# Second expert stage of a two-block network: down weights loaded with neighbouring rows in one partition, gate and up columns read with a stride

## What is computed

```python
def _moe_swiglu(u, w_router, w_gate, w_up, w_down):       # 256 tokens, 8 experts, top 2
    ...                                                    # tokens sorted by expert
    h = silu(ragged_dot(xs, w_gate, group_sizes)) * ragged_dot(xs, w_up, group_sizes)
    ys = ragged_dot(h, w_down, group_sizes) * top_w
    ...                                                    # summed back by token
```

## Time and profile before

| | us |
|---|---|
| timed runs, median of 3 (lowest, highest) | 2250.08 (2250.03, 2257.03) |
| profiled execution, its own time | 2249.02 |
| its span, first to last instruction | 2247.3 |
| TensorE busy (share) | 2081.7 (93%) |
| VectorE busy | 686.1 (31%) |
| ScalarE busy | 173.9 (8%) |
| GpSimd busy | 165.9 (7%) |
| mean granted TensorE clock | 0.939 |

### The profile page before, as it was taken

How to read it: one execution, slowest core, us unless ns; L and a number is a source line. 1 busy time by engine, 2 the same in 40 slices (tenths; PEclk the granted TensorE clock), 3 DMA queues, 4 the chain that set the end, 5 groups by cost and what they waited for, 6 DMA issues and landing times.

```text
span 2247.3 us, 72263 instructions
## 1 busy us (share of the span) xinstructions
PE 2081.7 (93%) x32971; PEld 1735.1 (77%) x32971; DVE 686.1 (31%) x1542; ACT 173.9 (8%) x280; POOL 165.9 (7%) x203
## 2 busy tenths in 40 slices
PE   6999998999999998998999989888999999989995
PEld 6899867777777776765877667478988989989893
DVE  5774533222222224235423441520110110101105
ACT  1000101000000000100000010020000101000000
POOL 8990000000000000000000000000000000000000
PEclk9977887999999998998999999979999999999997
DMA  9766455999999999334766633149999999999990
GB/s 310 287 242 245 164 201 182 386 393 393 395 395 394 392 395 391 137 113 142 260 251 231 243 131 132 57 174 393 376 379 396 381 384 382 383 393 372 380 396 28
DMA packets 310532, 656.16 MB, mean 292 GB/s; under 512 B 25620, under 2 KB 46644, under 8 KB 310452
## 3 DMA queue, kind: packets, MB, share of 16 engines
q1 hardware_dynamic: 300832, 647.02, 78.3%
q0 software_dynamic: 1456, 5.24, 0.7%
q10 hardware_dynamic: 8164, 2.73, 0.5%
HBM read 653.89 MB, written 1.05 MB: 291 GB/s over the span
## 4 chain that ended last, share of the span: by engine, by line
PE 73%; DMA 19%; DVE 4%; SPq 2%; issue 1%; ACTq 0%; ACT 0%; DVEq 0%
PE ps L1529 72%; DMA ring<-in_moe_w_up_dram 10%; DMA ring<-in_w_down_dram 9%; PE ps L1537 2%; SPq L416 1%; DMA ring<-in_w_ada_dram 1%; DVE hT L868 0%; SPq L329 0%; DMA arena<-in_gm_b_s_dram 0%; ACTq L555 0%; DVE x L941 0%; DVE stat L929 0%; DVE x L1335 0%; DVE x L912 0%; DVE x L910 0%
## 5 line engine op out<-in xcount | busy, mean ns | idle before, releaser
L1529 PE MATMUL ps<-arena,ring 128*64 128x80 f32 (+2 forms) x25216 | 887.9, 232 | 48.8 <-DMA ring<-in_moe_w_up_dram 46.2
L1529 PEld LDWEIGHTS ps<-arena,ring 128*64 128x64 f32 (+1 forms) x25216 | 872.8, 139 | 72.2 <-DMA ring<-in_moe_w_up_dram 50.3
L1529 PE MATMUL ps<-hT,ring 128*128 128x256 f32 x1616 | 363.7, 388 | 3.5 <-DVE stat L1472 1.9
L1529 PEld LDWEIGHTS ps<-hT,ring 128*128 128x128 f32 x1616 | 313.5, 195 | 50.4 <-issue 4.4
L1529 PE MATMUL ps<-ring,arena 128*64 128x512 f32 (+1 forms) x880 | 280.3, 609 | 16.4 <-DMA ring<-in_w_down_dram 15.1
L1529 PE MATMUL ps<-arena 128*128 128x128 f32 (+7 forms) x1296 | 232.9, 346 | 15.8 <-DVE arena L1387 5.6
L1529 PEld LDWEIGHTS ps<-ring,arena 128*64 128x64 f32 (+1 forms) x880 | 107.2, 162 | 171.1 <-issue 168.7
L1529 PEld LDWEIGHTS ps<-arena 128*128 128x128 f32 (+4 forms) x1296 | 160.4, 193 | 67.0 <-issue 41.6
L1274 DVE TENSOR_TENSOR arena<-arena,ps 128x160 f32<-128x160 f32 x88 | 28.3, 322 | 538.2 <-PE ps L1529 538.2
L1529 PEld LDWEIGHTS ps<-csT,ring 128*64 128x64 f32 x3072 | 141.9, 199 | 15.0 <-issue 11.5
L1529 PE MATMUL ps<-csT,ring 128*64 128x1 f32 x3072 | 142.7, 230 | 10.6 <-issue 7.2
(11 more groups left out here) (303 smaller groups left out, 860.6 us busy)
## 6 DMA issues: line engine op xcount, KB each, us to landing
ring<-in_moe_w_gate_dram SPq DMA_DIRECT2D x160, 512.0 KB, 10.0
ring<-in_moe_w_up_dram SPq DMA_DIRECT2D x160, 512.0 KB, 7.2
ring<-in_moe_w_down_dram SPq DMA_DIRECT2D x160, 512.0 KB, 10.2
ring<-in_w_gate_dram SPq DMA_DIRECT2D x32, 2048.0 KB, 20.0
ring<-in_w_up_dram SPq DMA_DIRECT2D x32, 2048.0 KB, 19.7
ring<-in_w_down_dram SPq DMA_DIRECT2D x32, 2048.0 KB, 18.9
ring<-in_w_in_dram SPq DMA_DIRECT2D x18, 2048.0 KB, 12.8
ring<-in_w_ada_dram SPq DMA_DIRECT2D x12, 2048.0 KB, 11.4
```

The source lines that it names most:

```text
L1529: ins = pe.matmul(*args, **kw)
```

## The change

The down matrix goes into the slot in another row order: partition p of a unit now holds the four neighbouring rows c0 + 4p to c0 + 4p + 3, which lie 16 KB in one piece in DRAM, and it is loaded in `SPANS` = 2 transfers of two rows (8 KB) per partition instead of four of one row. Hidden tile f is therefore the features 4q + f, q = 0 to 127, and so gate and up columns of that tile are taken 4 columns apart (16 bytes) from the slot, whose loading stays as it was. In the tail there are two rows per partition, loaded in one transfer as before, and the columns are 2 apart. The freeing of the down slot goes by halves: `FREES` falls from 9 to 7. The branch `second_all` gets the same order (`spread_tiles`).

```diff
-FREES = 2 * PIECES + 1
+SPANS = 2
+FREES = PIECES + 1 + SPANS
...
-        down_piece = [sem(f"down_piece{i}") for i in range(PIECES)]
+        down_piece = [sem(f"down_piece{i}") for i in range(SPANS)]
...
+            def row_spans(w, e, c0, n):
+                return w[bass.ds(e, 1), c0:c0 + n, :].rearrange("o (p k) n -> p (o k) n", p=P)
+
             def load_unit(e, c0, waits):
-                gate, up, down = expert_cols(wg, e, c0, CH), expert_cols(wu, e, c0, CH), expert_rows(wd, e, c0, CH)
+                gate, up, down = expert_cols(wg, e, c0, CH), expert_cols(wu, e, c0, CH), row_spans(wd, e, c0, CH)
...
-                for f in range(PIECES):
-                    sp.wait_ge(*waits(PIECES + 1 + f))
-                    sp.dma_start(down_w[:, f:f + 1, :], down[:, f:f + 1, :]).then_inc(down_piece[f], 16)
+                for h in range(SPANS):
+                    sp.wait_ge(*waits(PIECES + 1 + h))
+                    sp.dma_start(down_w[:, 2 * h:2 * h + 2, :], down[:, 2 * h:2 * h + 2, :]).then_inc(down_piece[h], 16)
...
-                sp.dma_start(tail_down_w, expert_rows(wd, e, c0, TAIL)).then_inc(tail_full["down"], 16)
+                sp.dma_start(tail_down_w, row_spans(wd, e, c0, TAIL)).then_inc(tail_full["down"], 16)
...
+            def column_span(w, f):
+                return w.rearrange("p k (q f) -> p k f q", q=P)[:, :, f, :]
...
-                                      gate_w[:, k, f * P + c * HALF:f * P + (c + 1) * HALF], xT[:, k, 0:cap],
+                                      column_span(gate_w, f)[:, k, c * HALF:(c + 1) * HALF], xT[:, k, 0:cap],
...
-                                          w[:, k, f * P + c * HALF:f * P + (c + 1) * HALF], xT[:, k, 0:cap],
+                                          column_span(w, f)[:, k, c * HALF:(c + 1) * HALF], xT[:, k, 0:cap],
...
-                    for f in range(PIECES):
-                        unit_ready([down_piece[f]], n)
-                        if f % 2 == 0:
-                            pe.wait_ge(q["hid_ready"], i * halves + u * 2 + (f // 2 + 1))
-                        down(down_w, f, False).then_inc(unit_free, 1)
+                    for h in range(SPANS):
+                        unit_ready([down_piece[h]], n)
+                        pe.wait_ge(q["hid_ready"], i * halves + u * 2 + (h + 1))
+                        down(down_w, 2 * h, False)
+                        down(down_w, 2 * h + 1, False).then_inc(unit_free, 1)
```

More of the change, by code:

```diff
@@ L1616, in hT_ready, with spread_tiles @@
                 pe.wait_ge(a_free, na[0])
+            def column_span(w, f):
+                return w.rearrange("p k (q f) -> p k f q", q=P)[:, :, f, :]
+            def spread_tiles(w, rhs, tiles, bank):
+                for i, f in enumerate(tiles):
+                    for k in range(KD):
+                        last = mm(ps[:, bank, i * T:(i + 1) * T], column_span(w, f)[:, k, :], rhs(k),
+                                  start=(k == 0), stop=(k == KD - 1))
+                return last
             def feature_major(w, rhs, tiles, bank, cols=lambda f: f * P, kt=KD, m=P):
@@ L1749, in _, with dense_in @@
             router(w_router, 36)
-            def dense_in(q, gate, up, n, i, per, j):
+            def dense_in(q, gate, up, n, i, per, j, tiles_of=feature_major):
                 for h in range(n // FU):
@@ L1755, in dense_in @@
                         pe.wait_ge(q["silu_done"], i * per + (j + h))
-                    feature_major(gate, h_rhs, (2 * h, 2 * h + 1), 4).then_inc(q["gate_full"], 1)
+                    tiles_of(gate, h_rhs, (2 * h, 2 * h + 1), 4).then_inc(q["gate_full"], 1)
                     if j + h:
                         pe.wait_ge(q["hid_ready"], i * per + (j + h))
-                    feature_major(up, h_rhs, (2 * h, 2 * h + 1), 5).then_inc(q["up_full"], 1)
+                    tiles_of(up, h_rhs, (2 * h, 2 * h + 1), 5).then_inc(q["up_full"], 1)
             def dense_down(q, w, n, i, per, j, unit, opens, closes):
@@ L1809, in second_all @@
                         unit_ready([up_block], i * UNITS + u, PIECES)
-                        dense_in(q, gate_w, up_w, CH, i, S2, 2 * u)
+                        dense_in(q, gate_w, up_w, CH, i, S2, 2 * u, spread_tiles)
                         free(PIECES + 1, unit_free)
                         unit_ready(down_piece, i * UNITS + u)
-                        dense_down(q, down_w, CH, i, S2, 2 * u, u, u == 0, False).then_inc(unit_free, PIECES)
+                        dense_down(q, down_w, CH, i, S2, 2 * u, u, u == 0, False).then_inc(unit_free, SPANS)
                     unit_ready([tail_full["gate"], tail_full["up"]], i)
-                    dense_in(q, tail_gate_w, tail_up_w, TAIL, i, S2, 2 * UNITS)
+                    dense_in(q, tail_gate_w, tail_up_w, TAIL, i, S2, 2 * UNITS, spread_tiles)
                     free(2, tail_free)
```

## The result

The changed kernel takes 2444.0 us (median of 4 runs, 2440.7 to 2444.8) against 2250.1 before: 1.085 times as long, 95% interval 1.083 to 1.088, 194 us slower. The forecast of 2246 us was wrong. The time lies where the first rival put it (2432 for a weight load twice as long), and 4 us beyond the range.

A forecast was written before the change was run, and what follows sets the result against it. Transfers were taken as the bound, TensorE nearly level with them. From 2249.0 us, packets took off 4, freeing, SP and strided loads added 0: 2245.0, or 2246 on the median's scale; range 2237 to 2440.

The forecast's parts named there:

- the first rival: Second expert stage: strided weight loads become TensorE's bound; doubled load gives 2432 us, chance 0.32; 1.5 times, 2285, chance 0.10.
- the strided weights: Gate and up weight loads on TensorE, columns 16 bytes apart: extra cost taken as hidden behind the product, 0 us.
- the slack: TensorE in the second expert stage: 7.3 us per expert that it can lose before the stage slows down.
- middle case: First rival's smaller size: strided load 1.5 times as long, 44.4 ns per instruction, 2285 us; chance 0.10.
- The packets: Down matrix transfers: two rows in one 8 KB packet save 10 ns per pair, 6.7 us, of which 4 us arrive.
- Freeing by halves: Down slot reloaded in two 1 MB halves instead of four 512 KB pieces: hidden by 3 us of margin, cost 0.
- SP's queue: SP issues two transfers fewer per unit, 80 in all, at 345 ns each: off the path, 0 us.
- The tail: Tail weights read with a stride of 8 bytes, two elements to a line: taken as unchanged in all cases.
- The second rival: Down transfers: the pair still travels as two 4 KB packets, or the gain only makes idle time; 2250 us, chance 0.13.

The follow-up runs named there:

- e2_stride: Kernel before with gate and up columns of a unit read 4 apart (2 in the tail), down matrix still loaded in four pieces of 4 KB rows; 2444.0 us.
- e7_full: Changed kernel with gate and up weights of units and tail loaded as one block of 128 columns instead of two of 64, strides kept; 3124.1 us.
- e8_narrow: Changed kernel with only 40 of the 80 token columns streamed in the gate and up products of units and tail; 2447.0 us in one run.

## Why the prediction was wrong

**The step that failed** is the last term of the sum, the strided weights, taken as hidden. I reasoned that a float32 column takes two cycles of the load already, and that this is time enough to reach another address. The runs fit 1.8 ns for each line of 16 bytes touched. With two elements to a line that is the 0.9 ns for each element of the contiguous load, which is why it looks as if it had room; with one element to a line it is twice as much. The load became 2.05 times as long (118 ns against 57.5), beyond the 1.17 from which it shows and the 1.38 from which the stage slows.

The Trainium skill, page "SBUF — State Buffer", section "Door 1: The DMA port swizzle", asks for at least two accesses to a line of 16 bytes; the runs agree, with 61 to 62 ns for a pair at stride 2 and 120 at stride 4. Its following sentence, which lets float32 stride four elements for free, doesn't hold here: two are all but free, three cost a half more, four the double.

**The rival's price** was right in kind. It had 58.8 ns for a strided instruction, 22.8 us per expert and 2432 us; measured were 60.1 ns, 24.7 us and 2444. TensorE's work on an expert grew by 32.5 us (from 82.1 to 114.6) where the rival had 30.1, and the slack took 7.9 off instead of 7.3. Its middle case, 44.4 ns at 1.5 times the load and 2285 us, came with stride 3: 43.7 ns and 2274. The bound 2440 of the range took the doubled load as the worst and left nothing for its pace to be a little above.

**The packets**: 10 ns for each pair was right. The rows of before continue to 309 ns for 8192 bytes, on 16 engines 424 GB/s, and 424 was measured; the packets' own records in the stage have 84, 159 and 309 ns for 2, 4 and 8 KB at their tenth percentile (87, 162 and 314 at the median). Of 6.7 us I let 4 arrive; 5.6 do in the run with contiguous columns (3.2 to 8.3 by its interval, so 4 and 6.7 both fit). In the changed kernel none does, since no wait for a transfer is left that it could shorten: `e2_stride`, without the longer packets, takes the same 2444 us.

**Freeing by halves and SP's queue**: nothing, as taken. **The slack**: 7.9 us against 7.3. **The tail** at stride 2: unchanged, as the rival had it. **The second rival**, that the pair travels as two packets, is refuted by the count.

## What to carry to other kernels

A layout that makes a transfer's rows longer is paid for where the slot is read: look up which stride it forces on the weight loads, in bytes, and keep two elements of a float32 weight operand within 16 bytes. Where the load is hidden behind its product, work out first how much longer it may get, and from there how much slack the engine has in a period; here that was a factor of 1.38, and any price of the size that was to be feared passed it. Pairs of rows gave the whole gain of the longer packets at no such price, and quadruples of rows, in two transfers of 8 KB, gave nothing more.

## What was not expected of the hardware

Loading 128 strided columns at a time (`e7_full`), TensorE was never idle, and yet its granted clock fell to 0.50, the 1.2 GHz level, in each stretch of strided loads, and came back to 1.00, the 2.4 GHz level, only within the down products behind it. The pace of the strided loads was about 234 ns both where the clock was 1.00 and where it was 0.50 (the rows above), so it isn't set by that clock. What suffers are the down products: on the timeline 34 of them take 2.48 us at 0.50, and 64 take 2.38 us at 1.00. An expert of the whole kernel took 200 us.

With halves of 64 columns and 80 moving ones the clock stayed at 1.00 in the stage. With 40 moving columns (`e8_narrow`) it did so in three experts of eight; in the other five its mean was 0.81 to 0.94, and those took up to 3.9 us longer. TensorE was busy throughout there too. Why the clock falls under a busy TensorE stays open.
